# RWKV-7 window scan: the triangle products head by head, and the group-norm mean ahead of the first triangle

## The chip, the cores and the metric

The kernel runs on one core of one Trainium2 chip. The metric is the device time of one execution in microseconds (us). The core's engines run side by side and meet at semaphores: PE (TensorE, matmuls and, as PEld, their weight loads), DVE (VectorE), ACT (ScalarE), POOL (GpSimd) and SP, which issues most DMAs.

## The reference, cut to what matters

The program is one inference step of four interleaved layers on 512 latent and 128 context tokens: Fourier mixing, short convolution, RWKV-7 time mixing and latent attention, each followed by an MLP. The change touches only the last stage of the RWKV-7 mixer. There, for each of 16 heads of width 64 and both directions of time, a state is carried over the tokens, and the result of both directions is normalised per head:

```python
def step(s, inp):
    rt, wt, kt, vt, kkt, at = inp
    sa = jnp.einsum('bhvk,bhk->bhv', s, -kkt)
    s = s * wt[:, :, None, :] + sa[..., None] * (kkt * at)[:, :, None, :] + vt[..., None] * kt[:, :, None, :]
    return s, jnp.einsum('bhvk,bhk->bhv', s, rt)
...
y = outs[0] + outs[1]
mean = jnp.mean(y, axis=-1, keepdims=True)
var = jnp.mean(jnp.square(y - mean), axis=-1, keepdims=True)
y = ((y - mean) * lax.rsqrt(var + GN_EPS)).reshape(b, n, d) * ln_g + ln_b
```

## The kernel before, in words

Features lie on the 128 partitions, tokens on the free axis. A tile `m` of 128 features holds two heads, head 0 on partitions 0 to 63 and head 1 on partitions 64 to 127. There are 8 tiles, and each has two directions `d`; the pass `q = 2m + d` works on one tile in one direction, so there are 16 passes, one after the other. Tile 0 is written out in the program; tiles 1 to 7 run in a hardware loop.

A pass cuts the 640 tokens into five windows of 128. In PE's function `windows(m, d, norm)` it goes through these steps:

- `triangles(w)`, for each window: products of the rows of one head among themselves. Each head has three matmuls, with 128, 256 and 128 moving columns, all in 4-byte floats and all contracting over the head's own 64 partitions. Head 0 writes one bank of `pu`, head 1 the next. The windows alternate between two pairs of banks.
- DVE answers every triangle with a select (`copy_predicated`, L2235) of the 128x1024 result into `at_`. Triangle w+2 waits for the select of window w (semaphore `tri_ready`), since it writes the same banks.
- `tokens(w)`, for each window: four 128x128 transposes through PE, which ACT copies out (L1551, L1552).
- `pairs(kind)`: six chains of small matmuls, whose results ACT and DVE take turns to copy out (DVE at L2255).
- The states of the windows, the outputs `y` (L1079 is the last of them), and DVE's copy or addition of `y` into `yb` (L2291 for d = 0, L2289 for d = 1), which raises the semaphore `y_read`.

The group norm of tile m-1 is spread over the pass (m, 0): `norm_mean` on PE (two matmuls over 320 columns, L906, after `y_read`), `centre` on DVE (L2195, subtracts the mean; it waits for `gn_sum`, which `norm_mean` raises), the square on ACT (L1536), `norm_square` on PE (L906 again, after the last triangle), the root on ACT (L1541), and `finish` on DVE (from L2202, a reciprocal first).

Order is fixed by how the code is written; each engine works through its own list. Before the change PE does `triangles(0)` and then `norm_mean`; DVE does the select of window 0 and then `centre`. At the head of a pass DVE also makes four block transposes (L2228).

Of the kernel before, what the change touches and what calls it, by code (L numbers as in the profile page):

```python
# [65 lines left out]
def halves(ap):  # L66

    return ap.rearrange("p (h n) -> p h n", h=2)


def build(nc, a, layers=(0, 1, 2, 3)):
    ctx = ExitStack()
    with ctx:
# [175 lines left out]
        pu = ctx.enter_context(nc.psum_tensor("pu", [P, 2, 2, 512], F32))  # L249
# [363 lines left out]
        def _(pe):  # L613
            tile = [0]
            slab = [0]
            norm = [0]
# [220 lines left out]
            def rwkv():  # L837
# [81 lines left out]
                def gate(m):  # L919
# [5 lines left out]
                    mm.then_inc(g_done, 1)  # L925

                windows(0, 0, None)
                windows(0, 1, None)
                with pe.Fori(1, KD) as m:
                    windows(m, 0, (norm_mean, norm_square, gate))  # L930
                    windows(m, 1, None)
# [5 lines left out]
            def windows(m, d, norm):  # L937

                q = 2 * m + d
                first = isinstance(q, int) and q == 0  # L940
# [17 lines left out]
                def triangles(w):  # L958

                    if w >= 2:  # L960
                        pe.wait_ge(tri_ready, NW * q + w - 1)
                    elif not first:
                        pe.wait_ge(qt_ready, q)
                    c = slice(w * P, (w + 1) * P)
                    by_head = [(slice(64 * h, 64 * h + 64), pu[:, w % 2, h, :]) for h in range(2)]
                    for r, out in by_head:
                        pe.matmul(out[:, 0:P], ar[d][r, w, 0, :], bk[d][r, 0, c], start=True, stop=True, skip_group_check=True)  # L967
                    for r, out in by_head:
                        pe.matmul(out[:, P:3 * P], bk[d][r, 1, c], ar[d][r, w, :, :].rearrange("p c n -> p (c n)"), start=True,
                                  stop=True, skip_group_check=True)  # L970
                    for r, out in by_head:
                        mm = pe.matmul(out[:, 3 * P:4 * P], bk[d][r, 0, c], ar[d][r, w, 1, :], start=True, stop=True,
                                       skip_group_check=True)
                    mm.then_inc(tri_done, 1)
# [43 lines left out]
                              skip_group_check=True).then_inc(s_done, 1)  # L1018

                pe.wait_ge(b3_landed[d], 48 * (m + 1))  # L1020
                v = vr if d else vd
                triangles(0)
                if norm:
                    norm[0](m)
                if d:
                    pe.wait_ge(vrev_ready, m + 1)
                else:
                    pe.wait_ge(v_landed, 16 * (m + 1))
                tokens(0)
                triangles(1)  # L1030
                tokens(1)
                triangles(2)
                tokens(2)
                triangles(3)
# [669 lines left out]
        def _(dve):  # L1704
            tile = [0]
            norm = [0]
# [350 lines left out]
            def rwkv():  # L2057
# [134 lines left out]
                def centre(m):  # L2192

                    dve.wait_ge(gn_sum, m)
                    dve.scalar_tensor_tensor(halves(ta[:, :]), aux[:, 2:4, 0:HT], -1.0 / HS, halves(yb[:, :]), ALU.mult, ALU.add  # L2195
                                             ).then_inc(gn_centred, 1)
# [23 lines left out]
                def scan_tile(m, first):  # L2220
                    col = bass.ds(m, 1)
                    for d in range(2):
                        q = 2 * m + d
                        lat0, ctx = (1, 0) if d else (0, NL)
                        dve.wait_ge(b3_landed[d], 48 * (m + 1))
                        for b in range(4):
                            rr = slice(32 * b, 32 * b + 32)
                            op = dve.transpose(dt_[rr, :, rr], xc[d][rr, :, :])  # L2228
                        op.then_inc(dt_ready, 1)
                        for w in range(NW):  # L2230
                            if w == 1 and d == 0 and not first:
                                centre(m)
                            dve.wait_ge(tri_done, NW * q + w + 1)
                            dve.sem_inc(tri_seen, 1)
                            dve.copy_predicated(at_[:, w, :, :, :].rearrange("p h c n -> p h (c n)"),  # L2235
                                                mask[:, :].unsqueeze(1).to_broadcast([P, 2, 4 * P]),
                                                pu[:, w % 2, :, :]).then_inc(tri_ready, 1)
                        if d == 0:
                            dve.wait_ge(v_landed, 16 * (m + 1))
                            dve.tensor_copy(vr[:, :], vd[:, ::-1]).then_inc(vrev_ready, 1)  # L2240
                            dve.wait_ge(s0_landed, 16 * (m + 1))
                        em, ec = (ewin[:, col, d, j, :].rearrange("p m w -> p (m w)") for j in range(2))
                        for h in range(2):
                            r = slice(64 * h, 64 * h + 64)
                            op = dve.tensor_scalar(sb_[r, 0, r], s0[r, d, :], em[r, lat0:lat0 + 1], None, ALU.mult)
                        op.then_inc(s_ready, 1)
                        dve.tensor_tensor(ecm[:, :], ec[:, lat0:lat0 + NL - 1], em[:, lat0 + 1:lat0 + NL], ALU.mult)
                        if d == 0 and not first:
                            finish(m)
                        for i in range(3):  # L2250
                            for w in range(NW):
                                n = 3 * NW + i * NW + w
                                c = w == ctx
                                dve.wait_ge(pair_done, 6 * NW * q + n + 1)
                                dve.tensor_tensor(zz[:, w, c:2, :, :].rearrange("p c h n -> p (c h n)"),  # L2255
                                                  pu[:, (n + 2) % 4 // 2, n % 2, c * P:2 * P],
                                                  rp[:, w, c:2, :, :].rearrange("p c h n -> p (c h n)"), ALU.add
                                                  ).then_inc(pair_dve, 1)

                        dve.wait_ge(mt_done, q + 1)  # L2260
                        dve.tensor_tensor(mt[:, :, :], pt[:, 0:(NL - 1) * P].rearrange("p (w n) -> p w n", n=P),
                                          ident[:, :].unsqueeze(1).to_broadcast([P, NL - 1, P]), ALU.add).then_inc(mt_ready, 1)
                        dve.drain()

                        def state(i):

                            dve.wait_ge(s_done, (NL - 1) * q + i + 1)
                            dve.scalar_tensor_tensor(sb_[:, i + 1, :], pm[:, i * P:(i + 1) * P], ecm[:, i:i + 1], blk[:, :],
                                                     ALU.mult, ALU.mult).then_inc(s_ready, 1)

                        state(0)
                        if d == 0:
                            dve.wait_ge(so_stored, 16 * m + 16)
                        for h in range(2):
                            r = slice(64 * h, 64 * h + 64)
                            op = dve.tensor_scalar(so[r, d, :], pm[r, (NL - 1) * P + 64 * h:(NL - 1) * P + 64 * h + 64],
                                                   ec[r, ctx:ctx + 1], None, ALU.mult)
                        op.then_inc(so_ready, 1)
                        dve.wait_ge(qt_done, q + 1)
                        dve.tensor_tensor(qt[:, :, :], pu[:, 0, 0, :].rearrange("p (w n) -> p w n", n=P),  # L2280
                                          ar[d][:, lat0:lat0 + NL, 1, :], ALU.add).then_inc(qt_ready, 1)
                        state(1)
                        state(2)
                        dve.wait_ge(y_done, q + 1)
                        for p, e, b in ((0, LAT, 0), (LAT, T, 1)):
                            y = st[:, b, 0:e - p]
                            if d:
                                out = yb[:, T - e:T - p]
                                op = dve.tensor_tensor(out[:, ::-1], y, out[:, ::-1], ALU.add)  # L2289
                            else:  # L2290
                                op = dve.tensor_copy(yb[:, p:e], y)  # L2291
                        op.then_inc(y_read, 1)

                scan_tile(0, True)
                with dve.Fori(1, KD) as m:
                    scan_tile(m, False)
# [380 lines left out]
```

## Time and profile before

| | us |
|---|---|
| median of 3 runs | 4247.48 |
| lowest and highest | 4244.51 and 4252.07 |
| the profiled execution, its own time | 4247.48 |
| its span in the trace | 4245.7 |
| PE busy in the span | 3612.9 (85%) |
| DVE busy | 2219.2 (52%) |
| ACT busy | 1277.5 (30%) |
| POOL busy | 1211.6 (29%) |

Busy time of PE counts records that overlap, and their ends are modelled, so it is read here from the starts of records: how far one lies behind the one before. A 4-byte float matmul appears as two records, its two passes, and each has a weight load of its own (PEld). So "x4" on a line with two matmuls is two passes for each. The rows name a source line and the tiles (out<-in), and then the shape: 64*128 means that 64 partitions are contracted into 128 output rows, 128*128 that all 128 partitions are.

### The profile page before, as it was taken

The page shows a single profiled execution, that of the slowest core. Times are in us where ns is not written, and L with a number is a line of the kernel's source. Part 1 is how long each engine was busy: PE and PEld are TensorE (multiplying, and loading weights), DVE is VectorE, ACT ScalarE, POOL GpSimd, SP SyncE. Part 2 cuts the span into 40 slices and gives each one's busy share as a digit, 9 for nine tenths or more (in the row PEclk, how much of TensorE's full clock was granted, in tenths as well). Part 3 has the DMA queues.
Part 4 walks back from the last instruction along what each step waited for, and adds up shares of the span by engine and source line. Part 5 has one row for each costly group of instructions (what it writes and reads, how often), then busy time and mean ns, then how long its engine had stood idle before and what let it go on. Part 6 is the DMA issues. An engine that isn't in the chain of part 4 may idle for free.

```text
span 4245.7 us, 65574 instructions
## 1 busy us (share of the span) xinstructions
PE 3612.9 (85%) x23794; PEld 3315.1 (78%) x23794; DVE 2219.2 (52%) x3621; ACT 1277.5 (30%) x2273; POOL 1211.6 (29%) x505
## 2 busy tenths in 40 slices
PE   5899999999999479545079999899997777799998
PEld 3689998989999369433078888899996665589998
DVE  8544675644564682577766767445644532252113
ACT  2243224234223212344022233342224122253223
POOL 0354335546334213000000000354334200155334
PEclk9999999999999679655589999999998887799999
DMA  5334553334544113233121121234443100033223
GB/s 218 129 125 159 180 186 129 109 105 134 179 158 148 56 49 122 104 104 106 55 96 49 53 63 36 95 130 168 173 144 102 60 15 0 25 119 119 75 76 114
DMA packets 170348, 453.20 MB, mean 107 GB/s; under 512 B 56208, under 2 KB 63824, under 8 KB 169424
## 3 DMA queue, kind: packets, MB, share of 16 engines
q1 hardware_dynamic: 164288, 436.88, 30.6%
q10 hardware_dynamic: 5904, 14.20, 0.9%
q8 instruction: 102, 1.67, 0.2%
q14 instruction: 54, 0.44, 0.0%
HBM read 412.59 MB, written 38.44 MB: 106 GB/s over the span
## 4 chain that ended last, share of the span: by engine, by line
issue 77%; POOL 13%; PE 9%; POOLq 1%; DVE 0%; DMA 0%; DVEq 0%; ACT 0%; ACTq 0%; SPq 0%
POOL ws L602 13%; PE pu L641 4%; PE pu L646 2%; PE pu L661 1%; PE pu L670 1%; POOLq L605 0%; POOLq L601 0%; POOLq L602 0%; DMA wr<-in_w_slabs 0%; PE aux L689 0%; DVE aux L1744 0%; DVE aux L1727 0%; DVE x L1749 0%; DVE pu L1744 0%; PE aux L696 0%
## 5 line engine op out<-in xcount | busy, mean ns | idle before, releaser
L602 POOL TENSOR_TENSOR ws<-wr,ws 128x1024 fp32r<-128x1024 f32 x501 | 1211.4, 2419 | 3011.9 <-ACT ws L1241 3011.3
L1241 ACT ACTIVATE ws<-wr 128x1024 fp32r<-128x1024 f32 x501 | 529.1, 1056 | 1099.3 <-PE pu L646 441.4
L641 PE MATMUL pu<-hs,ws 128*128 128x320 f32 x3776 | 584.2, 312 | 45.1 <-DVE hs L2093 45.1
L641 PEld LDWEIGHTS pu<-hs,ws 128*128 128x128 f32 x3776 | 564.5, 190 | 51.1 <-issue 29.9
L661 PE MATMUL pu<-hs,ws 128*128 128x320 f32 x2368 | 396.2, 318 | 42.2 <-DVE hs L1766 19.0
L641 PE MATMUL pu<-fs,ws 128*128 128x320 f32 x2592 | 402.1, 312 | 17.2 <-DVE fs L2093 17.2
L661 PEld LDWEIGHTS pu<-hs,ws 128*128 128x128 f32 x2368 | 362.8, 193 | 65.5 <-issue 23.8
L641 PEld LDWEIGHTS pu<-fs,ws 128*128 128x128 f32 x2592 | 387.8, 190 | 21.5 <-DVE fs L2093 21.5
L661 PE MATMUL pu<-fs,ws 128*128 128x320 f32 x2304 | 376.5, 315 | 17.7 <-DVE acc L2430 11.2
L1892 DVE SCALAR_TENSOR_TENSOR mjunk<-mr,aux 128x1024 f32<-128x1024 f32 x284 | 335.6, 1219 | 79.4 <-DMA mr<-in_m_slabs 54.7
L661 PEld LDWEIGHTS pu<-fs,ws 128*128 128x128 f32 x2304 | 349.9, 191 | 33.9 <-issue 12.3
L646 PE MATMUL pu<-hs,ws 128*128 128x320 f32 x1888 | 299.3, 311 | 0.0
L646 PEld LDWEIGHTS pu<-hs,ws 128*128 128x128 f32 x1888 | 285.1, 190 | 0.0
L670 PE MATMUL pu<-hs,ws 128*128 128x320 f32 x1184 | 210.8, 320 | 0.0
L646 PE MATMUL pu<-fs,ws 128*128 128x320 f32 x1296 | 205.4, 311 | 0.0
L670 PE MATMUL pu<-fs,ws 128*128 128x320 f32 x1152 | 196.9, 312 | 0.0
L646 PEld LDWEIGHTS pu<-fs,ws 128*128 128x128 f32 x1296 | 195.8, 190 | 0.0
L1631 ACT ACTIVATE relu<-pu 128x640 f32<-128x640 f32 x92 | 64.8, 705 | 429.5 <-PE pu L646 429.5
L670 PEld LDWEIGHTS pu<-hs,ws 128*128 128x128 f32 x1184 | 186.9, 194 | 8.9 <-issue 7.3
L670 PEld LDWEIGHTS pu<-fs,ws 128*128 128x128 f32 x1152 | 176.2, 189 | 3.5 <-POOL ws L602 2.1
L1551 ACT ACTIVATE rhs<-aux 128x128 f32<-128x128 f32 x80 | 22.3, 279 | 415.5 <-PE aux L955 415.5
L967 PE MATMUL pu<-bk,ar 64*128 64x128 f32 x320 | 40.1, 327 | 118.0 <-DMA xc<-inv_d 109.7
(299 smaller groups left out, 4795.5 us busy)
## 6 DMA issues: line engine op xcount, KB each, us to landing
wr<-in_w_slabs SPq DMA_DIRECT2D x501, 512.0 KB, 3.3
mr<-in_m_slabs SPq DMA_DIRECT2D x167, 512.0 KB, 5.2
ar_d<-ar SPq DMA_DIRECT2D x16, 640.0 KB, 3.0
bk_d<-bk SPq DMA_DIRECT2D x16, 640.0 KB, 4.3
ar<-ar_d SPq DMA_DIRECT2D x16, 640.0 KB, 4.0
bk<-bk_d SPq DMA_DIRECT2D x16, 640.0 KB, 5.2
mx<-in_m_slabs SPq DMA_DIRECT2D x16, 512.0 KB, 6.7
rkv_d<-relu ACTq DMA_DIRECT2D x24, 320.0 KB, 2.2
```

What stands on the lines that cost most here:

```text
L602: pool.tensor_tensor(ws[s % 2][:, 1, :], wr[:, s % 2, :], ws[s % 2][:, 0, :].bitcast(F32), ALU.subtract).then_inc(lo_ready, 1)
L641: pe.matmul(pu[:, t % 2, h, 0:HT], ws[s % 2][:, 0, k * P:(k + 1) * P], src[:, k, part, h * HT:(h + 1) * HT], start=(k + part == 0), stop=F ...
L646: mm = pe.matmul(pu[:, t % 2, h, 0:HT], ws[s % 2][:, 1, k * P:(k + 1) * P], src[:, k, 0, h * HT:(h + 1) * HT], start=False, stop=(k == KD ...
L661: pe.matmul(pu[:, t % 2, h, 0:HT], ws[s % 2][:, 0, k * P:(k + 1) * P], src[:, k, part, h * HT:(h + 1) * HT], start=(k + part == 0), stop=F ...
L670: mm = pe.matmul(pu[:, t % 2, h, 0:HT], ws[s % 2][:, 1, k * P:(k + 1) * P], src[:, k, 0, h * HT:(h + 1) * HT], start=False, stop=(k == KD ...
L967: pe.matmul(out[:, 0:P], ar[d][r, w, 0, :], bk[d][r, 0, c], start=True, stop=True, skip_group_check=True)
L1241: act.activation(ws[s % 2][:, 0, :], wr[:, s % 2, :], ACT.Copy).then_inc(hi_ready, 1)
L1551: act.activation(rhs[:, w, 0, :, :].rearrange("p h n -> p (h n)"), b[:, 0:P], ACT.Copy)
L1631: act.activation(halves(relu[:, j, :]), pu[:, t % 2, :, 0:HT], ACT.Relu).then_inc(relu_ready, 1)
L1892: op = dve.scalar_tensor_tensor(mjunk[:, g, :], at, 0.5, vector[:, g, :], ALU.mult, ALU.mult, accum_out=modt[:, col, g:g + 1].rearrange("p ...
```

## The change

It has three parts. In `triangles` the three matmuls of head 0 now come first and then the three of head 1, where before the heads took turns at each of the three products. In `windows`, `norm[0](m)`, which is `norm_mean`, stands ahead of `triangles(0)` instead of behind it; this concerns the passes with d = 0 of tiles 1 to 7. In DVE's `scan_tile`, `centre(m)` stands ahead of the selects of all windows instead of between those of windows 0 and 1. Code behind the edit moves up by one line.

```diff
@@ triangles @@
-                    by_head = [(slice(64 * h, 64 * h + 64), pu[:, w % 2, h, :]) for h in range(2)]
-                    for r, out in by_head:
+                    for h in range(2):
+                        r = slice(64 * h, 64 * h + 64)
+                        out = pu[:, w % 2, h, :]
                         pe.matmul(out[:, 0:P], ar[d][r, w, 0, :], bk[d][r, 0, c], start=True, stop=True, skip_group_check=True)
-                    for r, out in by_head:
                         pe.matmul(out[:, P:3 * P], bk[d][r, 1, c], ar[d][r, w, :, :].rearrange("p c n -> p (c n)"), start=True,
                                   stop=True, skip_group_check=True)
-                    for r, out in by_head:
                         mm = pe.matmul(out[:, 3 * P:4 * P], bk[d][r, 0, c], ar[d][r, w, 1, :], start=True, stop=True,
                                        skip_group_check=True)
                     mm.then_inc(tri_done, 1)
@@ windows @@
                 pe.wait_ge(b3_landed[d], 48 * (m + 1))
+                if norm:
+                    norm[0](m)
                 v = vr if d else vd
                 triangles(0)
-                if norm:
-                    norm[0](m)
@@ scan_tile @@
                         op.then_inc(dt_ready, 1)
+                        if d == 0 and not first:
+                            centre(m)
                         for w in range(NW):
-                            if w == 1 and d == 0 and not first:
-                                centre(m)
                             dve.wait_ge(tri_done, NW * q + w + 1)
```

On PE, at the head of the loop over tiles 1 to 7 (`ar` and `bk` are the operands of the triangles, `yb` the outputs of the tile before, `ident` the identity of the transposes), the kernel before has this:

```order
L1079 MATMUL aux<-qt_145,sb__144 128x128 x4
L929 UNCONDITIONAL_BRANCH
L929 ISA
L963 REGISTER_ALU
L967 MATMUL pu<-bk_0_132,ar_0_130 128x128 x2
L969 MATMUL pu<-ar_0_130,bk_0_132 128x256 x2
L972 MATMUL pu<-ar_0_130,bk_0_132 128x128 x2
L906 MATMUL aux<-yb_143,blk_104 128x320 x2
L1028 REGISTER_ALU
L955 MATMUL aux<-ident_65,ar_0_130 128x128
```

The changed kernel has this at the same place:

```order
L1078 MATMUL aux<-qt_145,sb__144 128x128 x4
L929 UNCONDITIONAL_BRANCH
L929 ISA
L911 REGISTER_ALU
L906 MATMUL aux<-yb_143,blk_104 128x320 x2
L968 MATMUL pu<-bk_0_132,ar_0_130 128x128
L969 MATMUL pu<-ar_0_130,bk_0_132 128x256
L971 MATMUL pu<-ar_0_130,bk_0_132 128x128
L968 MATMUL pu<-bk_0_132,ar_0_130 128x128
L969 MATMUL pu<-ar_0_130,bk_0_132 128x256
L971 MATMUL pu<-ar_0_130,bk_0_132 128x128
L955 MATMUL aux<-ident_65,ar_0_130 128x128
```

The mean (L906) has moved from behind the first triangle to ahead of it, and each "x2", which was one matmul of each head in turn, has become two separate rows, the first three of head 0 and the next three of head 1.

On DVE, at the head of the same pass (`xc` the inverted blocks, `at_` what the selects fill, `ta` the centred outputs), the kernel before has this:

```order
L2228 STREAM_TRANSPOSE dt__137<-xc_134 32x10x32 x4
L2233 ISA
L2235 COPY_PREDICATED at__142<-mask,pu 128x1024
L2195 SCALAR_TENSOR_TENSOR ta<-aux,yb 128x640
L2233 REGISTER_ALU
L2235 COPY_PREDICATED at__142<-mask,pu 128x1024
```

The changed kernel has this:

```order
L2227 STREAM_TRANSPOSE dt__137<-xc_134 32x10x32 x4
L2194 SCALAR_TENSOR_TENSOR ta<-aux,yb 128x640
L2232 ISA
L2234 COPY_PREDICATED at__142<-mask,pu 128x1024
L2232 REGISTER_ALU
L2234 COPY_PREDICATED at__142<-mask,pu 128x1024
```

The centring has moved ahead of the first select; nothing else moves on DVE.

## Rows read from the trace of the kernel before

**Rows 1.** One round of the loop (both directions), busy time by engine
```profile
core 0: us, PE busy (x) PEld busy (x) DVE busy (x) ACT busy (x) POOL busy (x), PEclk, DMA share, GB/s
2206.70:2273.30 66.60, 63.87 (x597) 57.34 (x596) 45.80 (x80) 20.36 (x54) 0.00 (x0) 1.00 0.18 56
```

**Rows 2.** All records of L967: duration ns min/median/max, first and last start us
```profile
L967 PE MATMUL pu<-bk,ar x320: 272/373/579, 2141.6 to 2649.8; 64*128 64x128 f32 x160
```

**Rows 3.** Timeline of PE, head of pass (1, 0): start us, us, records
```profile
2206.71 0.49 PE L967 MATMUL pu<-bk,ar 64*128 64x128 f32 x4
2207.04 0.60 PE L969 MATMUL pu<-ar,bk 64*128 64x256 f32 x4
2207.47 0.39 PE L972 MATMUL pu<-ar,bk 64*128 64x128 f32 x4
2207.79 1.34 PE L906 MATMUL aux<-yb,blk 128*128 128x320 f32 x4
2208.97 0.27 PE L955 MATMUL aux<-ident,ar 128*128 128x128 f32 x1
...
2209.50 0.49 PE L967 MATMUL pu<-bk,ar 64*128 64x128 f32 x4
...
2211.16 0.49 PE L967 MATMUL pu<-bk,ar 64*128 64x128 f32 x4
...
2213.06 0.49 PE L967 MATMUL pu<-bk,ar 64*128 64x128 f32 x4 [0.16 <-DVE at__142 L2235]
...
2215.16 0.49 PE L967 MATMUL pu<-bk,ar 64*128 64x128 f32 x4
...
2216.24 1.34 PE L906 MATMUL aux<-root,blk 128*128 128x320 f32 x4
```

**Rows 4.** Timeline of DVE, the same stretch
```profile
2206.82 0.89 DVE L2289 TENSOR_TENSOR yb<-aux,yb 128x512 f32<-128x512 f32 x2 [1.76 <-PE aux L1079]
2207.63 2.04 DVE L2228 STREAM_TRANSPOSE dt__137<-xc 32x320 f32<-32x320 f32 x4
2209.70 1.35 DVE L2235 COPY_PREDICATED at__142<-mask,pu 128x1024 f32<-128x1024 uint32 x1
2210.92 0.83 DVE L2195 SCALAR_TENSOR_TENSOR ta<-aux,yb 128x640 f32<-128x640 f32 x1
...
2216.46 1.34 DVE L2235 COPY_PREDICATED at__142<-mask,pu 128x1024 f32<-128x1024 uint32 x1 [0.75 <-PE pu L972]
...
2218.71 4.15 DVE L2202 RECIPROCAL rstd<-root 128x640 f32<-128x640 f32 x1
```

**Rows 5.** Timeline of PE, head of pass (1, 1)
```profile
2241.66 0.49 PE L967 MATMUL pu<-bk,ar 64*128 64x128 f32 x4
...
2243.36 0.49 PE L967 MATMUL pu<-bk,ar 64*128 64x128 f32 x4
...
2246.00 0.49 PE L967 MATMUL pu<-bk,ar 64*128 64x128 f32 x4 [0.91 <-DVE at__142 L2235]
...
2250.84 1.16 PE L999 MATMUL pu<-dt__137,at__142 128*128 128x128 f32 x8
```

**Rows 6.** Timeline of PE cut off 0.11 us into one triangle
```profile
2211.16 0.38 PE L967 MATMUL pu<-bk,ar 64*128 64x128 f32 x2
```

**Rows 7.** Timeline of PE, the pair products of pass (1, 0)
```profile
2217.42 2.39 PE L999 MATMUL pu<-dt__137,at__142 128*128 128x128 f32 x20
...
2228.34 0.43 PE L999 MATMUL pu<-rp,gt 128*128 128x64 f32 x2 [1.20 <-DVE zz L2255]
```

**Rows 8.** Timeline of PE's weight loads in the stage before, clock 0.5
```profile
1842.23 2.21 PEld L891 LDWEIGHTS aux<-bk,ar 64*128 64x128 f32 x20 [2.65 <-ACT blocks L1530]
...
1845.07 0.33 PEld L861 LDWEIGHTS pu<-tw,l 64*128 64x128 f32 x1 [0.20 <-issue]
1845.60 0.33 PEld L861 LDWEIGHTS pu<-tw,l 64*128 64x128 f32 x1 [0.20 <-issue]
```

**Rows 9.** Timeline of PE, first triangle and what follows it, pass (0, 0)
```profile
2141.57 0.80 PE L967 MATMUL pu<-bk,ar 64*128 64x128 f32 x4 [109.67 <-DMA xc<-inv_d]
...
2143.58 0.47 PE L955 MATMUL aux<-ident,ar 128*128 128x128 f32 x1
```

## The prediction

> **What bounds the kernel now.** I began with the count of records of the triangles, to find the stretch that the change touches. L967 has 320 records between 2141.6 and 2649.8 us; with two heads and two passes a triangle that is 80 triangles, five windows in 16 passes [rows 2]. Next I took busy times by engine over one round of the loop, two passes: in 66.6 us PE is busy 63.9, DVE 45.8, ACT 20.4, and the granted clock is 1.00, which is 2.4 GHz [rows 1]. PE is the first suspect, but its records overlap, so the third view is its timeline, read by starts. In pass (1, 0) the triangles start at 2206.71, 2209.50, 2211.16, 2213.06 and 2215.16, and only one of them shows a wait, 0.16 us for DVE's select [rows 3]. In pass (1, 1) there is one, 0.91 us, at the third triangle [rows 5]. Over that head of a pass PE sets the time and DVE nearly keeps up: a select takes 1.35 us and the step from triangle to triangle is 1.66 us (2209.50 to 2211.16) [rows 3, 4]. Last I looked at how the six matmuls of a triangle lie to each other, since that is what the change rearranges.
>
> **Part 1, the order of the heads.** In the view cut off 0.11 us into a triangle, two records of L967 have started and together cover 0.38 us [rows 6]; one alone has a median of 0.373 us [rows 2]. So the first passes of head 0 and head 1 start within 0.01 us of each other: they contract over different halves of the partitions, and they run at the same time. The column rates say the same. On all 128 partitions, 20 passes of 128 columns fill 2.39 us; less the 0.27 us that a last record lasts, that is 2.12 / 19 = 0.112 us a pass [rows 3, 7]. The four passes of 256 columns of a triangle begin at 2207.04, and L972 follows at 2207.47: 0.43 us, where four passes of 256 columns one after another would take 4 x 2 x 0.107 = 0.86 (0.107 is 0.43 / 4, the time of 128 columns in a paired pass of 256) [rows 3].
>
> One after another, what does a head cost? Its six passes move 2 x (128 + 256 + 128) = 1024 columns, 8 x 0.107 = 0.86 us. Now both heads share these 0.86 us; a whole triangle, from start to the next instruction, is 2207.79 - 2206.71 = 1.08, the rest being its lead-in and change-over [rows 3]. In the changed order head 1 can start beside head 0's last pass only, as it now starts beside head 0's first. All later passes of head 1 come behind. The addition is 0.86 - 0.107 = 0.76 us, and a triangle becomes 1.84 us. That passes on the same half really are serial is shown in the stage before, at half the clock: two loads in a row of L861, 64 partitions, 320 columns, start 0.53 us apart, or 0.213 us for 128 columns; L891, whose heads take turns, brings 20 loads in 2.21 - 0.33 us, 19 steps of 0.099 us [rows 8]. That is half, at the same clock. The bounds: nothing if the order didn't matter, and 0.87 if head 1 gets no overlap at the hand-over either. I take 0.76.
>
> Is a weight load hidden when the next matmul uses the same half? In L861 the load lasts 0.33 us and yet the step of 0.53 us is twice the 0.27 that the columns alone take at full clock (320 x 0.107 / 128), so the load costs nothing (0.53 / 320 is 1.67 ns a column, two periods of 1.2 GHz) [rows 8]. The Trainium skill says otherwise for packed tiles: its page "TensorE: Matmul & The Clock Gate", section "The mechanism" of Part 3, has it that weight loads overlap with matmuls in flight "only when row_grp differs". By that rule every pass but each head's first would show its load; the trace here contradicts it. The sum by it would be that of rival B below, 4387 us.
>
> **Part 2, the mean ahead of triangle 0.** This touches seven passes, (1, 0) to (7, 0). Now PE fills the wait for `y_read` with triangle 0: DVE's addition runs from 2206.82 to 2207.71, and the mean starts at 2207.79, just as the triangle is through [rows 3, 4]. In the new order PE waits from 2206.71 until about 2207.82 and does nothing. Queued behind the waiting mean are all triangles, and behind those DVE's selects. The mean takes 2208.97 - 2207.79 = 1.18 us; with 0.09 for the change from full to half partitions (the four transposes take 2209.50 - 2208.97 = 0.53, of which four passes are 0.44), triangle 0 starts at 2209.1 instead of 2206.71.
>
> **Part 3, `centre` ahead of the selects.** It takes 0.83 us on DVE [rows 4]. After the change the mean is there at 2209.2, the block transposes end at 2209.67, so `centre` runs to 2210.5. Triangle 0 is done only at 2209.1 + 1.84 + 0.2 = 2211.1. So it hides fully in DVE's idle time. It costs nothing and gains nothing, since `finish` can't start before the root, which hangs on `norm_square` behind the last triangle; the reciprocal at 2218.71 follows the last select without a wait [rows 4].
>
> **The sum, pass by pass.** A step from triangle to triangle becomes 1.66 + 0.76 = 2.42 us. A select now starts 2216.46 - 2215.16 = 1.30 us after its triangle's start, so it will start 2.06 after it and be done at 3.41 [rows 3, 4]. The triangle that needs it is two steps on, at 4.84, so no triangle waits for DVE any more.
>
> - d = 0, tiles 1 to 7: triangle 0 at 2209.1, then 2211.5, 2213.9, 2216.4; the last step has two groups of transposes, 2215.16 - 2213.06 = 2.10, and becomes 2.86: 2219.2. It ends at 2221.1, where it ended at 2216.24 before: +4.8 us [rows 3]. (As a check: 5 x 0.76 = 3.8, and 1.1 of waiting for `y_read`, less about 0.2 of waits that go.) Seven times: 33.7.
> - d = 1, all tiles: triangles at 2241.66, 2244.1, 2246.5, 2248.9, 2251.8, end 2253.6, before 2250.84: +2.8 us (3.8 less the 0.91 wait that goes) [rows 5]. Eight times: 22.4.
> - Pass (0, 0): no mean; its first triangle runs at the lower clock, 2143.58 - 2141.57 = 2.01 us [rows 9]. The clock rises at its own time, and the added work is 3.8 us at full speed: +3.8.
>
> The last select, the square sum and all that follows hang on the last triangle and move with it; the wait of 1.20 us for DVE at the pair products comes from `finish`, which moves too [rows 7]. Sum 33.7 + 22.4 + 3.8 = 59.9 us. The profiled execution took 4247.48, which is also the median: 4307.4 us, +1.4%. The bounds of the addition give its range: with 0.87 it is 80 x 0.11 = 8.8 more, 4316; with 0.65, should passes at the hand-over of heads mix better than the rows show, 4299.
>
> **Rivals.**
>
> A. Only the moves count. If PE ran the three matmuls of a head as fast as it now runs pairs, a triangle would stay at 1.08 us. Then tile 1's triangle 0 starts at 2209.1, the fifth at about 2216.2 instead of 2215.16, +1.0 us seven times: 4254.5, within 0.2%. Against it are the two records that start together. 5%.
>
> B. Weight loads exposed. A first pass that has to wait for its load is longer than a later one: 0.373 against 0.272, so 0.10 us [rows 2]. Ten passes of a triangle would pay it: 80 x 1.0 = 80 us on top, about 4387. Against it is L861 with a load in the shadow of the same half [rows 8]. 3%.
>
> C. The other side, faster: DVE's selects come closer together once `centre` no longer stands between those of windows 0 and 1. The 0.16 us at the fourth triangle and some of what surrounds it, at most 0.5 us a pass, would be won in seven passes, 3.5 us: 4244, if triangles keep their length and triangle 0 is not missed at the start. It decides only where the select, not PE, is late; with 1.84 us a triangle it never is. 2%, and even then within 0.2% rather than beyond.
>
> D. The pairing is lost only in part, say half: 4275 to 4295. The records give no reason for it. 5%.
>
> **How the numbers follow.** The forecast has 85%, own range 4299 to 4317; A 5, B 3, C 2, D 5. The likeliest is 4307. For 8 in 10 I take 4296 to 4319. Faster or slower by over 0.2% (8.5 us) is about what a measurement of this kernel can tell from no change. Slower: the forecast, B and D, 93%; within 0.2%: A and most of C, 6%; faster: 1%.
>
> **What would show it.** In the changed profile a triangle lasts 1.84 us from its first record to the next line, and a view cut off 0.11 us into one has a single record, not two. The step between triangles is about 2.4 us with no wait for DVE; L906 on `yb` shows a wait of about 1.1 us for DVE's addition at the head of seven passes; DVE shows waits of about 1 us for PE before most selects; `centre` ends before the first select. A round of the loop takes 66.6 + 7.6 = 74.2 us. The forecast is wrong if the triangles stay near 1.1 us (A), or if they come to 2.8 us (B).

## The result and the profile after

Over five runs on each side the changed kernel took 4285.76 us (4274.28 to 4289.52) against 4247.48 (4244.46 to 4252.59). The ratio is 1.0081, interval 1.0061 to 1.0100: slower, as forecast, but by 34 us (26 to 42) by this ratio and not by 60. The measured median lies below the range of 4296 to 4319. The profiled execution took 4273.91, with a span of 4272.1.

The stretch that the change touches, from the start of the first triangle to that of the last, is 2137.0 to 2677.0 = 540.0 us; before it was 2141.6 to 2649.5 = 508.0. That is +32.0. The whole profiled execution lost only 4273.91 - 4247.48 = 26.4: what lies ahead of the first triangle took 4.6 us less than in the profile before and what lies behind the last 1.1 less. There the two programs are the same, and the five times before alone spread over 8 us. So the +32.0 of the stretch is what has to be explained.

Timeline of PE in the changed kernel, from the last outputs of pass (0, 1) over the head of pass (1, 0), and the end of its fifth triangle; start us, us, records:

```profile
2208.39 1.16 PE L1078 MATMUL aux<-qt,sb__144 128*128 128x128 f32 x8
2210.53 1.34 PE L906 MATMUL aux<-yb,blk 128*128 128x320 f32 x4 [0.98 <-DVE yb L2288]
2211.80 0.49 PE L968 MATMUL pu<-bk,ar 64*128 64x128 f32 x2
2212.12 0.38 PE L969 MATMUL pu<-ar,bk 64*128 64x256 f32 x1
2212.13 0.37 PE L968 MATMUL pu<-bk,ar 64*128 64x128 f32 x1
2212.34 0.38 PE L969 MATMUL pu<-ar,bk 64*128 64x256 f32 x1
2212.34 0.27 PE L968 MATMUL pu<-bk,ar 64*128 64x128 f32 x1
2212.46 0.38 PE L969 MATMUL pu<-ar,bk 64*128 64x256 f32 x1
2212.56 0.38 PE L971 MATMUL pu<-ar,bk 64*128 64x128 f32 x2
2212.67 0.38 PE L969 MATMUL pu<-ar,bk 64*128 64x256 f32 x1
2212.89 0.38 PE L971 MATMUL pu<-ar,bk 64*128 64x128 f32 x2
2213.20 0.33 PE L955 MATMUL aux<-ident,ar 128*128 128x128 f32 x1
...
2220.19 0.49 PE L968 MATMUL pu<-bk,ar 64*128 64x128 f32 x2
...
2221.59 1.34 PE L906 MATMUL aux<-root,blk 128*128 128x320 f32 x4
```

Follow the lines. The program has six passes of head 0 and then six of head 1: 968 968 969 969 971 971, twice. The trace has 968 968 969 and then 968 again, at 2212.13, ahead of head 0's second 969 at 2212.34. That second 968 is head 1's first pass, 0.33 us behind head 0's. From there the two heads run side by side, until head 0 is through and head 1 finishes alone. The triangle takes 2213.20 - 2211.80 = 1.40 us; before it was 1.08 [rows 3], and the forecast was 1.84.

DVE at the same place, with the additions, the block transposes, the centring and the first selects:

```profile
2209.58 0.89 DVE L2288 TENSOR_TENSOR yb<-aux,yb 128x512 f32<-128x512 f32 x2 [1.76 <-PE aux L1078]
2210.39 2.04 DVE L2227 STREAM_TRANSPOSE dt__137<-xc 32x320 f32<-32x320 f32 x4
2212.46 0.82 DVE L2194 SCALAR_TENSOR_TENSOR ta<-aux,yb 128x640 f32<-128x640 f32 x1
2213.42 1.32 DVE L2234 COPY_PREDICATED at__142<-mask,pu 128x1024 f32<-128x1024 uint32 x1
2215.41 1.33 DVE L2234 COPY_PREDICATED at__142<-mask,pu 128x1024 f32<-128x1024 uint32 x1 [0.67 <-PE pu L971]
```

The centring ends before the first select could start, and from the second select on DVE waits for PE. This answers to [rows 4].

The odd pass (1, 1), whose head stood in [rows 5]:

```profile
2246.99 0.49 PE L968 MATMUL pu<-bk,ar 64*128 64x128 f32 x2
...
2248.98 0.48 PE L968 MATMUL pu<-bk,ar 64*128 64x128 f32 x2
...
2251.36 0.49 PE L968 MATMUL pu<-bk,ar 64*128 64x128 f32 x2 [0.32 <-DVE at__142 L2234]
...
2257.18 1.05 PE L998 MATMUL pu<-dt__137,at__142 128*128 128x128 f32 x7
```

Each triangle again has a second group of L968 behind its first L969, as above; those lines are left out. The wait of 0.91 us at the third triangle has shrunk to 0.32, and the stretch from the first triangle to the pair products takes 2257.18 - 2246.99 = 10.19 us where it took 9.18.

Last, the granted clock. Busy times and PEclk, in the columns of [rows 1], over the first 15 us from the first triangle, the kernel before and then the changed one:

```profile
2141.50:2156.50 15.00, 14.47 (x108) 12.07 (x109) 9.61 (x13) 5.34 (x16) 0.00 (x0) 0.79 0.33 104
```

```profile
2136.90:2151.90 15.00, 14.94 (x67) 12.70 (x68) 7.09 (x8) 2.28 (x8) 0.00 (x0) 0.50 0.26 85
```

Before, the granted clock rose from 1.2 to 2.4 GHz 6.3 us after the first triangle (the mean of 0.79 says the same: 6.3 us at 0.5 and 8.7 at 1.0); now it rises after 16.8 us, behind the end of this window. From the first triangle of pass (0, 0) to that of pass (1, 0) it was 2206.71 - 2141.57 = 65.1 us, and is 2211.80 - 2136.96 = 74.8. Each later round takes 70.22 us against 66.65.

### The profile page after: what moved, and what is told of

Its sections match the earlier page's. It is cut to its first block, busy times and chain, and to the rows that moved or that the text cites. A ratio compares the mean times of both kernels' runs of the same rounds, so it can differ in the third digit from the quotient of the medians.

```text
span 4272.1 us, 65574 instructions
## 1 busy us (share of the span) xinstructions
PE 3637.6 (85%) x23794; PEld 3338.0 (78%) x23794; DVE 2221.2 (52%) x3621; ACT 1278.0 (30%) x2273; POOL 1211.3 (28%) x505
## 4 chain that ended last, share of the span: by engine, by line
issue 77%; POOL 13%; PE 9%; POOLq 1%; DVE 0%; DMA 0%; DVEq 0%; ACT 0%; ACTq 0%; SPq 0%
POOL ws L602 13%; PE pu L641 4%; PE pu L646 2%; PE pu L661 1%; PE pu L670 1%; POOLq L605 0%; POOLq L601 0%; POOLq L602 0%; DMA wr<-in_w_slabs 0%; PE aux L689 0%; DVE aux L1743 0%; DVE aux L1726 0%; DVE x L1748 0%; DVE pu L1743 0%; PE aux L696 0%
## 5 line engine op out<-in xcount | busy, mean ns | idle before, releaser
L968 PE MATMUL pu<-bk,ar 64*128 64x128 f32 x320 | 68.1, 333 | 112.1 <-DMA xc<-inv_d 109.4
```

## The experiments

My theory after the result: PE runs the matmuls of the two halves of the partitions as two streams, and what the new order costs is only the lag with which the second starts ("lag"). Its rivals were that the moves (the mean and the centring) carry the loss, and, for the size of the lag, several rules. Each experiment kernel was compared with the kernel before on the same chip. "Round" is the steady time from a tile's first triangle to the next tile's, 66.65 us in the kernel before. Experiments e4 to e7, e9 and e11 are one execution each; since single executions of the kernel before spread over 17 us and more on these chips, they are read by their profiles.

**e1, order only.** Triangles as in the changed kernel, the rest as before.

```diff
-                    for r, out in by_head:          # three such loops, one product each
-                        pe.matmul(...)
+                    for h in range(2):
+                        pe.matmul(...)              # the three products of one head
```

> Triangles head by head, the mean and the centring at their old places. Theory 'lag' (head 1's passes start 0.33 us behind head 0's and then run beside them, so a triangle is 1.08 + 0.33 = 1.40 us): pass with d=1 +1.0 us, pass with d=0 +1.4 us, first pass 3 to 7 us by when the clock rises; sum 21 to 25 us, about 4270. Rival 'the order costs what the moves leave' (the moves cost 3 us a pass and the order little): under 10 us.

Measured: 4273.43 against 4251.28, ratio 1.0054 (1.0040 to 1.0069), +23 us, as the lag theory had it (21 to 25). Triangle 1.40, round 69.03 (+2.4); the clock rose 19.5 us after the first triangle.

**e2, moves only.** The two `+` and `-` pairs of `windows` and `scan_tile` from the change, `triangles` as before.

> The mean ahead of triangle 0 and the centring ahead of the selects, the heads taking turns as before. Theory 'lag': the wait for the output addition shows in front of L906 (about 1 us), less the waits for DVE that go: +1.0 us in each of seven passes, +7 us, 4254. Rival 'the moves carry the loss': +20 us or more.

Measured: 4258.03, ratio 1.0020 (1.0010 to 1.0030), +8.5 us. Round 67.62 (+0.97), clock up after 3.7 us. PE at the head of the pass, with the mean and the first triangle:

```profile
2212.09 1.34 PE L906 MATMUL aux<-yb,blk 128*128 128x320 f32 x4 [0.98 <-DVE yb L2289]
2213.36 0.49 PE L967 MATMUL pu<-bk,ar 64*128 64x128 f32 x4
2213.69 0.60 PE L969 MATMUL pu<-ar,bk 64*128 64x256 f32 x4
2214.12 0.39 PE L972 MATMUL pu<-ar,bk 64*128 64x128 f32 x4
2214.44 0.33 PE L955 MATMUL aux<-ident,ar 128*128 128x128 f32 x1
```

The triangle is at its old 1.08 us: the moves do nothing to it.

**e3, the changed kernel again.** No edit.

> The changed kernel once more, beside its parts. Sum of the parts: +28 to +33 us, about 4278. If the clock in the first pass of the scan rises 10 us later than in the kernel before (as in the changed profile) again, it belongs to the change; if it rises elsewhere, it is chance.

Measured: 4284.58, ratio 1.0078 (1.0062 to 1.0095). The parts give 1.0054 + 0.0020 = 1.0074: within the intervals they add up. Round 70.22, +3.57, where the parts give 2.38 + 0.97 = 3.35. The rest is a wait that each part alone saves and that both together can save only once: the step from the third to the fourth triangle is 1.90 us in [rows 3] and 1.66 without the wait for the select. The clock rose after 15.1 us; the late rise came again.

**e4, centring only**, one profile:

```diff
+                        if d == 0 and not first:
+                            centre(m)
                         for w in range(NW):
-                            if w == 1 and d == 0 and not first:
-                                centre(m)
```

> Only the centring is moved, ahead of the select of window 0. Both theories: select 0 starts 0.8 us later (about 2.8 us instead of 2.0 after the triangle's end), triangle 2 waits 0.8 us for it, triangle 3 no longer waits: +0.5 us in seven passes, +3 us, not to be told from none in one run; it is read in the profile.

Round 67.07, +0.4. The third triangle of pass (1, 0):

```profile
2211.63 0.49 PE L967 MATMUL pu<-bk,ar 64*128 64x128 f32 x4 [0.57 <-DVE at__142 L2235]
```

The centring delays select 0, and triangle 2 waits for it, as expected, though 0.57 us and not 0.8.

**e11, the mean only** ahead, centring between the selects as before, one profile.

> The kernel before, with only the mean ahead of triangle 0; the centring stays between the selects of windows 0 and 1, the heads take turns. The two moves together cost 0.97 us a round (e2), the centring alone 0.45 (e4). If the costs were independent this one would be 0.5 us; by the wait for the output addition I expect 1.0 to 1.3 us a round, since the centring stands in DVE's idle time in e2 and between two selects here.

Round 67.62, the same +0.97 as with both moves, and just under the 1.0 to 1.3 that I expected. So the mean carries it all; the centring costs something only where PE is not already late.

**e5, wide product first**, head by head:

```diff
                     for h in range(2):
-                        pe.matmul(out[:, 0:P], ...)          # 128 columns
                         pe.matmul(out[:, P:3 * P], ...)      # 256 columns
+                        pe.matmul(out[:, 0:P], ...)
                         mm = pe.matmul(out[:, 3 * P:4 * P], ...)
```

> Head by head as in e1, but with the 256-column product first in each head. Lag theory, by passes or by instructions left: head 1 starts with head 0's third pass, which now comes after two passes of 256 columns, so 0.54 us behind instead of 0.33, and a triangle is 1.62 us. Rival 'a fixed time': lag 0.33, triangle 1.40. Rival 'serial after all, the first triangles were special': 1.84.

Timeline of PE, one triangle (L968 is now the wide product, L970 and L971 the narrow ones):

```profile
2328.52 0.70 PE L968 MATMUL pu<-ar,bk 64*128 64x256 f32 x2
2329.05 0.27 PE L970 MATMUL pu<-bk,ar 64*128 64x128 f32 x1
2329.06 0.48 PE L968 MATMUL pu<-ar,bk 64*128 64x256 f32 x1
...
2330.13 0.33 PE L955 MATMUL aux<-ident,ar 128*128 128x128 f32 x1
```

Head 0's third pass starts at 2329.05 and head 1's first right behind, 0.54 us after the start; the triangle takes 1.61. It isn't a fixed time. The round is 70.74 us, the one execution took 4291.0.

**e6, four narrow products**, head by head; the wide one is cut in two:

```diff
-                        pe.matmul(out[:, P:3 * P], bk[d][r, 1, c], ar[d][r, w, :, :]...)
+                        pe.matmul(out[:, P:2 * P], bk[d][r, 1, c], ar[d][r, w, 0, :], ...)
+                        pe.matmul(out[:, 2 * P:3 * P], bk[d][r, 1, c], ar[d][r, w, 1, :], ...)
```

> Head by head, with the 256-column product cut into two of 128 columns, so each head has four matmuls, 8 passes of 128 columns. Theory 'from the front' (head 1 starts with head 0's third pass): lag 0.33 us, triangle 1.40. Theory 'from the back' (head 1 starts once about six of head 0's queued instructions are left, 12 before, 16 now): head 1 starts with head 0's fifth pass, lag 0.54 us, triangle 1.62.

```profile
2328.71 0.48 PE L968 MATMUL pu<-bk,ar 64*128 64x128 f32 x2
2329.03 0.38 PE L969 MATMUL pu<-ar,bk 64*128 64x128 f32 x2
2329.26 0.27 PE L970 MATMUL pu<-ar,bk 64*128 64x128 f32 x1
2329.26 0.37 PE L968 MATMUL pu<-bk,ar 64*128 64x128 f32 x1
...
2330.35 0.33 PE L955 MATMUL aux<-ident,ar 128*128 128x128 f32 x1
```

Head 1's first pass (the second L968 line) comes with head 0's fifth (L970), 0.55 us after the start; the triangle takes 1.64. So what counts is how much of head 0 is still to go, not how much has gone. Three of its eight passes are left behind the one just started; in the changed kernel three of six. The round is 71.00 us, the one execution took 4288.11.

**e7, two then one**: two products of each head, then the third of each.

```diff
                     for r, out in by_head:
                         pe.matmul(out[:, 0:P], ...)
-                    for r, out in by_head:
                         pe.matmul(out[:, P:3 * P], ...)
                     for r, out in by_head:
                         mm = pe.matmul(out[:, 3 * P:4 * P], ...)
```

> Two products of head 0, two of head 1, then the third of head 0 and the third of head 1. Theory 'from the front': head 1 starts with head 0's third pass, 0.33 us behind, triangle 1.3 to 1.4. Theory 'from the back' (eight instructions of head 0 ahead, six may be left): head 1 starts right behind head 0's first pass, at most 0.11 us, triangle 1.1 to 1.2 us.

```profile
2310.51 0.50 PE L967 MATMUL pu<-bk,ar 64*128 64x128 f32 x4
2310.84 0.61 PE L968 MATMUL pu<-ar,bk 64*128 64x256 f32 x4
2311.27 0.40 PE L971 MATMUL pu<-ar,bk 64*128 64x128 f32 x4
2311.60 0.33 PE L955 MATMUL aux<-ident,ar 128*128 128x128 f32 x1
```

The triangle takes 1.09 us and the round 66.65, as before the change; the one execution took 4250.59. Head 0's four passes leave three behind the first, and head 1 starts at once (the L967 line holds two passes of each head and covers 0.50 us; in [rows 3] it is 0.49). Two by two in the program, the heads run as if they took turns.

**e9, the first pass in turns**: the changed kernel, but `if first:` the old order.

> The changed kernel, but in pass (0, 0) alone the heads take turns as before; the other 75 triangles are head by head. Theory 'the lagging order keeps the clock low at the start of the scan': the clock rises 3 to 7 us after the first triangle instead of 15 to 20, the first ten triangles take 66 to 68 us instead of 74 to 75, the later rounds stay at 70.2 us. Rival 'the late rise is chance or comes from elsewhere': it rises at 15 us or more again, and the first round stays over 72 us.

```profile
2147.80:2162.80 15.00, 14.50 (x115) 12.38 (x115) 9.80 (x14) 5.69 (x18) 0.00 (x0) 0.84 0.33 111
```

The clock rose after 4.8 us, the first round was 67.8 us, the later ones 70.22. The 66 to 68 us expected hold.

**e10, the first pass head by head**: the kernel before, but `if first:` the new order, five triangles of 80.

> The kernel before, with the head by head order in pass (0, 0) alone, five triangles. Theory 'clock': the rise comes 15 to 20 us after the first triangle, and the first round takes 72 to 74 us instead of 65: five triangles cost 7 to 8 us, where five lags of 0.33 us at full clock are 1.6. Rival 'no effect on the clock': rise after 3 to 7 us, cost 2 to 3 us.

```profile
2139.90:2154.90 15.00, 14.94 (x67) 12.70 (x68) 7.15 (x8) 2.28 (x8) 0.00 (x0) 0.50 0.25 81
```

The clock rose after 15.0 us; first round 70.7 against 65.1, later rounds unchanged. Measured: 4251.73 against 4246.81; the ratio is 1.0015 (1.0003 to 1.0027), 1 to 11 us. The profile's 5.6 us is less than the 7 to 8 that I expected, but over three times the 1.6 of five lags at full clock.

**e8, block transposes early**: a version that beats both. The kernel before, with DVE's transposes for the next pass made in its waits at the end of this one.

```diff
-                        dve.wait_ge(b3_landed[d], 48 * (m + 1))
-                        for b in range(4):
-                            ...
                         state(1)
+                        turn(m + d, 1 - d, (0, 1))     # two of the four block transposes of the next pass
                         state(2)
+                        turn(m + d, 1 - d, (2, 3))     # the other two, then dt_ready
                         dve.wait_ge(y_done, q + 1)
...
+                sp.sem_inc(b3_landed[0], 48)           # on SP: the last turn has no next tile
```

The comments are mine. The four transposes of the very first pass are made once ahead of tile 0.

> The kernel before, with DVE's four block transposes (2.04 us at the head of each pass) made ahead for the next pass, two of them before the last state and two before the outputs, where DVE waits 1.09 and 1.76 us. Theory 'select 0 is late in the kernel before': the 0.91 us wait of triangle 2 (d=1) and 0.2 to 0.4 us of waits (d=0) go, 9 to 10 us in all, 4238 to 4242. Rival: the transposes push the last state or the output copy by 0.2 to 0.5 us a pass, and nothing is won: 4245 to 4255.

Measured: 4236.69 against 4249.16, ratio 0.9962 (0.9947 to 0.9976), faster by 16 us (10 to 23). DVE at the end of a pass, with the two pairs of transposes in what were waits of 1.09 and 1.76 us:

```profile
2206.23 1.00 DVE L2227 STREAM_TRANSPOSE dt__137<-xc 32x320 f32<-32x320 f32 x2
2207.41 0.35 DVE L2274 SCALAR_TENSOR_TENSOR sb__144<-aux,ecm,blk 128x128 f32<-128x128 f32 x1 [0.17 <-PE aux L1018]
2207.79 1.02 DVE L2227 STREAM_TRANSPOSE dt__137<-xc 32x320 f32<-32x320 f32 x2
2209.52 0.89 DVE L2297 TENSOR_TENSOR yb<-aux,yb 128x512 f32<-128x512 f32 x2 [0.71 <-PE aux L1080]
```

The state between them still starts 1.44 us after the one before, so nothing was pushed. The round is 65.43 us, -1.2, and the wait of 0.91 us at the third triangle of pass (1, 1) is gone. From the first triangle to the last the profile has 10.8 us less than before, which lies within the interval, near its lower end; the rest of the measured 16 has no place in the profile.

## Why the prediction was wrong

**The step that failed** is in part 1: "In the changed order head 1 can start beside head 0's last pass only ... All later passes of head 1 come behind. The addition is 0.86 - 0.107 = 0.76 us". It measured 0.325 (1.402 against 1.077). The rows were read rightly: the halves run in parallel [rows 6], and passes on one half are serial [rows 8], which the changed profile still shows within a head. What I took from nowhere was that PE starts matmuls strictly in the order of the program. It doesn't when they use different halves: it goes on past head 0's waiting passes and starts head 1's. The rows of the kernel before leave this open, because in all that I read program order and start order are the same. e5, e6 and e7 fit one rule for the size: head 1 starts once three passes of head 0 are left behind the one just started. That holds for 6, 8 and 4 passes a head, with lags of 0.33, 0.55 and 0.01 us, and for 6 with the wide one first, 0.54. Each pass has one load and one matmul here, so the runs don't tell whether passes or instructions count, and no run had a third stretch of one half behind the second.

The Trainium skill's page "TensorE: Matmul & The Clock Gate", section "The mechanism", has the same assumption: matmuls are monotone in program order in start and end, "strict FIFO, no reordering". The lines above contradict it. That section's other rule, on weight loads, I weighed as rival B. It falls too: head 0's two wide passes and the next one start at 2212.12, 2212.34 and 2212.56, so the two take 0.44 us, as they take 0.43 in [rows 3] with the heads in turns. No load shows between passes on one half.

**The mean ahead of triangle 0** (part 2) was right. PE shows a wait of 0.98 us for the addition, forecast 1.1, and the round loses 0.97 (e2, e11), forecast 1.0. Its seven passes make 6.8 us, and e2 measured 8.5 (4 to 13).

**The centring** (part 3) was right: beside the moved mean it costs nothing (e2 and e11 have the same round).

**The waits for DVE that go.** In d = 1 I let all 0.91 us go; with a smaller addition only 0.59 of it went. Pass by pass with 0.325: d = 1 is five times 0.325 less 0.6, measured 10.19 - 9.18 = +1.0 (forecast 2.8). In d = 0, from L1078 to the second L906, it is 2221.59 - 2208.39 = 13.20; before, L1079 started at 2205.62 and the second L906 at 2216.24, 10.62: +2.6 (forecast 4.8; the wait of about 1 us ahead of the mean is in both numbers).

**The first pass** I had at +3.8, saying "The clock rises at its own time". It does not: with the lagging order (head 1 starting late: the changed order, e5's or e6's) in that pass it rose 15.0 to 19.5 us after the first triangle in six profiles (the changed kernel twice, e1, e5, e6, e10), with the heads in turns, e7 included, 3.2 to 6.3 us in the seven others. e9 and e10 move it by the order of that pass alone. What in that order holds the clock down stays open. The pass cost +6.4 us in the changed profile (39.9 against 33.5). This error pointed the other way and hid 2.6 us of the first one; that is luck.

The sum of what was measured: 7 x 2.6 + 8 x 1.0 + 6.4 = 32.6, and the profile has 32.0.

**The signs.** Those of the moves came true, and a view cut off 0.11 us into a triangle has one record. That sign could not tell 1.84 us from 1.40, for head 1 starts only after 0.33. The waits of DVE for PE before the selects are 0.66 us, not 1, and the round is 70.22, not 74.2.

**The rivals.** A is out: the order alone costs 23 us (e1). C is out: the centring moved alone cost 0.4 us a round and won nothing (e4). D, "The pairing is lost only in part, say half", is what happened: the loss of the pairing is 0.325 of 0.76, or 43%. I gave it 5%, with "The records give no reason for it", and its 4275 to 4295 would have held the result. D named only a size, not how it would come about.

## What to carry to other kernels

Two streams of small matmuls on the two halves of the partitions run side by side, and in these runs PE found the second behind up to three waiting passes of the first. So two products of one half, two of the other and then one of each cost nothing here (e7, one execution), but longer runs of one half start the other late by whatever lies ahead of those three passes. A wait placed ahead of work that used to cover it costs nearly its whole length (0.98 us of wait, 0.97 a round). Work put into the waits of the partner engine can win, as the transposes did (e8, 10 to 23 us).

## What the runs showed of the hardware

- PE starts matmuls out of program order when they contract over different halves of the partitions: 0.33 us of lag for three products a head, 0.54 with the wide one first, 0.55 for four narrow ones, 0.01 for two. Once started, the second half is not slowed by the first: the triangle grows by 0.325 us, the lag and no more.
- The granted clock at the start of a stretch depended on how the matmuls lie, not only on PE being busy: over the first 15 us busy was 14.94 with the clock at 0.50, and 14.47 with 0.79. It rose after 15.0 us or more in all six profiles with the lagging order in the first pass and after 6.3 us or less in the seven others. Which quantity decides was not tested.
